# Attention in a hybrid decoder block: rounded values beside their remainder stationary, turned probabilities of two heads moving in two parts, sums turned back per four heads

## The chip, the cores and the metric

One Trainium2 chip, one core. The metric is device time in microseconds of one execution of the whole kernel, on the slowest (here the only) core. Three runs of the kernel before took 1873.67, 1875.36 and 1880.94 us; the median is 1875.36.

## What is computed

One decoder layer over a sequence of 1024 tokens and 1024 channels, in float32. Two token mixers run side by side: NSA (8 query heads, 2 key heads: a compressed branch, a branch over selected blocks, a sliding window of 512) and DSA (8 query heads, one key head, an indexer that keeps the top 256 keys). The change touches three of their products, probabilities times values, and how their result comes to the merge. The reference, cut to that:

```python
# NSA, per chunk of 64 queries; head dimension d = 64
p = masked_softmax(einsum('bqhgd,bqhkd->bqhgk', q_c, k_sel) * scale, sel_mask)      # "slc"
o_slc = einsum('bqhgk,bqhkd->bqhgd', p, v_sel)
p = masked_softmax(einsum('bqhgd,bkhd->bqhgk', q_c, kwin) * scale, win_mask)        # "win"
o_win = einsum('bqhgk,bkhd->bqhgd', p, vwin)
y_a = g0 * o_cmp + g1 * o_slc + g2 * o_win
# DSA                                                                             # "dsa"
y_b = einsum('bqhk,bqkd->bqhd', masked_softmax(einsum(q_c, k_sel) * scale, mask), v_sel)
merged = gate_a * (y_a @ w_branch_nsa) + gate_b * (y_b @ w_branch_dsa)
h = h + merged @ w_out
h = h + (silu(rmsnorm(h) @ w_gate) * (rmsnorm(h) @ w_up)) @ w_down
```

## The kernel before

The program is written per engine, with semaphores between them; nothing is planned by a tool, the order is that of the loops. It has these stages: normalise and project x (`z_step`, column groups idx, qb, cmp, win, qa, eight tiles of 128 tokens each), the indexer's scores and VectorE's bisection for the top keys, the merge gates' projection, the attention stage (about 495 to 946 us of the profiled span), the branch projections and merge (`m_step`, 16 steps of 24 products), the output projection, and the feed-forward part in two halves of the tokens.

**Number forms.** Wide products are made exact by splitting an operand: its rounding to the fast form F32R ("hi", always on ScalarE) and the remainder ("lo", on VectorE or GpSimd), each an operand of its own. `three` multiplies hi by hi, hi by lo and lo by hi. Where an operand is plain F32, one product is recorded as two passes.

**The attention stage** is one loop over steps u, run by each engine with its own part of each step. Its units are (branch, query tile i, head h), eight heads of a tile in a row: first all dsa tiles, then for each tile win and slc; 192 units. A unit works on n key blocks of 128: n = i + 1 for dsa and slc, at most 5 for win. In step u

- TensorE transposes the probabilities of unit u - 2 (`T_LAG`), 128 x 128 blocks, up to four into one of two PSUM banks (`group`, banks psT 0 and 1; line 1082 in `turn4`), makes the scores of unit u (lines 1141 and 1142, in psA), and multiplies the turned probabilities of unit u - 3 (`V_LAG`) by the values: probabilities stationary, 64 columns of values moving, plain F32 (line 1257), into an accumulator bank per tile (psT 2 and 3).
- ScalarE makes the exponential of unit u - 1 with its row sum (line 971) and copies the first turned bank out (`evac_p`, line 508); VectorE copies the second, if n > 4, and makes scores plus bias with the row minimum (line 1647, tile `s`).
- After the eighth head VectorE divides by the row sums (`scaled`, line 1675); for win and slc GpSimd adds that to the tile's y (line 798), which the compressed branch has begun (`cmp_out`, line 1682). At `Y_LAG` = 7 TensorE turns y, ScalarE rounds it (line 961), VectorE makes the remainder (line 1706): yTh and yTl, the operands of `m_step`.

`group` waits, before it writes a bank, until what was turned into it two groups ago has been taken out. The compressed branch (`cmp_tile`) runs along: its scores, softmax, output and the ranking of blocks (lines 1613 to 1630 on VectorE, the block bias on GpSimd) fall in fixed steps from slc of one tile to win of the next, and use the same two banks. In step 36 TensorE makes the compression products, 14.4 us in a row, in both kernels.

**Around it.** `z_evac` (ScalarE) takes each projection out of PSUM, `rope_cos` (GpSimd, line 705) multiplies by cosines, `rope` (VectorE, lines 1474 and 1479) by sines and adds. SyncE issues all loads in one order: queries two tiles ahead, the first weights of the merge (ring w2, two raw buffers, four split ones), then, after the last product and all banks taken, the gates, further weights and the gain. ScalarE splits two of these weights during the attention (`W2_AT`). `m_step(0)` runs near the end of the loop, the others after it; step m takes weight column block m // 2 and half m % 2 of the tokens.

## Time and profile before

| | us |
|---|---|
| median of three runs | 1875.36 |
| the runs | 1873.67 to 1880.94 |
| profiled execution: span from first to last instruction | 1870.0 |
| TensorE busy in the span | 1777.7 (95%) |
| VectorE | 837.2 (45%) |
| ScalarE | 672.4 (36%) |
| GpSimd | 584.2 (31%) |
| attention stage, first score to last value product | about 495 to 946 |

The profiled execution has no time of its own beside the runs; its span, 1870.0 us, is 5.4 under their median, and all rows below are read from it. How to read them: PE is TensorE's matmuls, PEld its weight loads, DVE is VectorE, ACT ScalarE, POOL GpSimd. A row of the timeline gives the start within the span, the duration, engine, line of the kernel, operation, output <- inputs, the form and how many such instructions are merged into the row; in brackets how long the engine had been idle and what released it. Matmuls are pipelined: a row's duration is longer than its distance to the next start, and the distance is what it costs. A window gives each engine's busy time in it and the granted TensorE clock as a share of 2.4 GHz (0.5 is the lower level, 1.2 GHz). The chain of waits is followed back from the last instruction, each step to what released it.

### The profile page before, as it was taken

The page shows a single profiled execution, that of the slowest core. Times are in us where ns is not written, and L with a number is a line of the kernel's source. Part 1 is how long each engine was busy: PE and PEld are TensorE (multiplying, and loading weights), DVE is VectorE, ACT ScalarE, POOL GpSimd, SP SyncE. Part 2 cuts the span into 40 slices and gives each one's busy share as a digit, 9 for nine tenths or more (in the row PEclk, how much of TensorE's full clock was granted, in tenths as well). Part 3 has the DMA queues.
Part 4 walks back from the last instruction along what each step waited for, and adds up shares of the span by engine and source line. Part 5 has one row for each costly group of instructions (what it writes and reads, how often), then busy time and mean ns, then how long its engine had stood idle before and what let it go on. Part 6 is the DMA issues. An engine that isn't in the chain of part 4 may idle for free.

```text
span 1870.0 us, 25106 instructions
## 1 busy us (share of the span) xinstructions
PE 1777.7 (95%) x9596; PEld 1526.2 (82%) x9596; DVE 837.2 (45%) x1796; ACT 672.4 (36%) x1310; POOL 584.2 (31%) x366
## 2 busy tenths in 40 slices
PE   6789979999999999999999989999999999999997
PEld 5667768888898999899988878888888888888886
DVE  6689788999135545566646322111131012311102
ACT  5543333221355467655522023322222223222222
POOL 3303233221220011321122024454454444544541
PEclk9899999999999989999999999999999999999999
DMA  5103232532422001001044223333333333433331
GB/s 175 45 12 103 80 96 86 174 90 74 113 64 113 24 29 30 12 17 31 1 130 141 80 85 96 91 100 103 90 102 102 101 90 90 140 105 93 101 102 68
DMA packets 179462, 158.01 MB, mean 84 GB/s; under 512 B 16912, under 2 KB 145936, under 8 KB 179088
## 3 DMA queue, kind: packets, MB, share of 16 engines
q1 hardware_dynamic: 179344, 156.41, 27.4%
q8 instruction: 77, 1.26, 0.3%
q14 instruction: 41, 0.34, 0.1%
HBM read 131.22 MB, written 25.17 MB: 84 GB/s over the span
## 4 chain that ended last, share of the span: by engine, by line
PE 84%; DVE 8%; ACT 3%; issue 2%; POOL 2%; DMA 1%; SPq 0%; DVEq 0%; ACTq 0%; POOLq 0%
PE psA L1075 18%; PE psA L1077 18%; PE psA L1076 18%; PE psT L1257 9%; PE psT L1082 7%; PE psA L1142 3%; PE psA L1141 3%; PE psT L1075 2%; PE psT L1077 2%; PE psT L1076 2%; POOL w_lo L319 1%; DVE rotated L1474 1%; DVE equal L1534 1%; DVE above L1534 1%; PE psT L1266 1%
## 5 line engine op out<-in xcount | busy, mean ns | idle before, releaser
L319 POOL TENSOR_TENSOR w_lo<-w_raw,w_hi 128x1024 fp32r<-128x1024 f32 (+2 forms) x184 | 453.6, 2479 | 657.4 <-ACT w_hi L314 657.4
L314 ACT CAST w_hi<-w_raw 128x1024 fp32r<-128x1024 f32 (+2 forms) x184 | 186.6, 1038 | 660.4 <-PE psA L1077 525.9
L1075 PE MATMUL psA<-hTh,w_hi 128*128 128x512 f32 x704 | 273.9, 389 | 0.2 <-POOL w_lo L319 0.2
L1076 PE MATMUL psA<-hTl,w_hi 128*128 128x512 f32 x704 | 273.9, 389 | 0.0
L1077 PE MATMUL psA<-hTh,w_lo 128*128 128x512 f32 x704 | 273.9, 389 | 0.0
L1820 DVE TENSOR_TENSOR act<-silu,psA 128x512 f32<-128x512 f32 x44 | 30.2, 687 | 393.5 <-ACT silu L1046 393.5
L971 ACT ACTIVATE p<-s,nmax 128x640 f32<-128x640 f32 (+7 forms) x192 | 144.0, 750 | 120.3 <-DVE nmax L1647 119.1
L1075 PEld LDWEIGHTS psA<-hTh,w_hi 128*128 128x128 f32 x704 | 132.1, 188 | 28.2 <-issue 0.6
L1076 PEld LDWEIGHTS psA<-hTl,w_hi 128*128 128x128 f32 x704 | 132.1, 188 | 27.4
L1077 PEld LDWEIGHTS psA<-hTh,w_lo 128*128 128x128 f32 x704 | 132.1, 188 | 27.2
L1082 PE MATMUL psT<-ident,p 128*128 128x128 f32 x816 | 131.0, 281 | 18.8 <-DVE yTl_dsa L1706 4.7
L1075 PE MATMUL psA<-w_hi,xTh 128*128 128x512 f32 (+2 forms) x320 | 123.5, 386 | 14.2 <-POOL w_lo L319 10.0
L1082 PEld LDWEIGHTS psT<-ident,p 128*128 128x128 f32 x816 | 98.4, 153 | 25.9 <-ACT p L971 6.4
L1077 PE MATMUL psA<-w_hi,xTl 128*128 128x512 f32 (+2 forms) x320 | 119.2, 372 | 0.0
L1076 PE MATMUL psA<-w_lo,xTh 128*128 128x512 f32 (+2 forms) x320 | 119.0, 372 | 0.0
L508 ACT COPY pT<-psT 128x512 f32<-128x512 f32 (+3 forms) x192 | 93.8, 488 | 20.6 <-PE psT L1082 20.1
L1075 PE MATMUL psA<-xTh,w_hi 128*128 128x512 f32 x256 | 100.0, 391 | 0.0
L1077 PE MATMUL psA<-xTh,w_lo 128*128 128x512 f32 x256 | 99.6, 389 | 0.0
L1076 PE MATMUL psA<-xTl,w_hi 128*128 128x512 f32 x256 | 99.6, 389 | 0.0
L1534 DVE TENSOR_SCALAR_CACHE_REDUCE equal<-score,bit_try 128x512 f32<-128x512 f32 (+2 forms) x93 | 93.8, 1008 | 0.0
L705 POOL TENSOR_TENSOR roped<-z,cosT 128x512 f32<-128x512 f32 (+3 forms) x48 | 40.7, 854 | 161.8 <-ACT z L846 96.1
L1075 PEld LDWEIGHTS psA<-w_hi,xTh 128*128 128x128 f32 x320 | 61.5, 192 | 26.1 <-POOL w_lo L319 12.6
(259 smaller groups left out, 3544.4 us busy)
## 6 DMA issues: line engine op xcount, KB each, us to landing
w_raw<-in_w_gate_dram SPq DMA_DIRECT2D x44, 512.0 KB, 3.8
w_raw<-in_w_up_dram SPq DMA_DIRECT2D x44, 512.0 KB, 3.9
w_raw<-in_w_down_dram SPq DMA_DIRECT2D x44, 512.0 KB, 3.8
w_raw<-in_w_in_dram SPq DMA_DIRECT2D x28, 512.0 KB, 3.9
scratch_gates<-gate_out SPq DMA_DIRECT2D x32, 256.0 KB, 2.9
gates<-scratch_gates SPq DMA_DIRECT2D x32, 256.0 KB, 4.1
xr<-in_x_dram SPq DMA_DIRECT2D x8, 512.0 KB, 4.9
scratch_q_dsa<-turned SPq DMA_DIRECT2D x8, 512.0 KB, 2.6
```

Of the source, the lines that this page charges most:

```text
L314: nc.scalar.copy(self.hi[n % RING][:, 0:u], self.raw[n % RAW][:, 0:u]).then_inc(self.hi_done, 1)
L319: nc.gpsimd.tensor_tensor(self.lo[n % RING][:, 0:u], self.raw[n % RAW][:, 0:u], self.hi[n % RING][:, 0:u].bitcast(F32), ALU.subtract).then ...
L508: copy(pT[v % 2][:, c0 // P:c1 // P, :].rearrange("p k t -> p (k t)"), psT[:, g6[key] % 2, 0:c1 - c0])\
L971: a_.activation(p_sb[v % PR][:, 0:n], s_sb[v % 2][:, 0:n], ACT.Exp, scale=-1.0, bias=nmax[:, BR[a], i, h:h + 1], accum_out=psum_p[:, BR[a] ...
L1075: pe.matmul(ps, ah, bh, start=first, stop=False)
L1076: pe.matmul(ps, ah, bl, start=False, stop=False)
L1077: mm = pe.matmul(ps, al, bh, start=False, stop=last)
L1082: mm = pe.transpose(bank[:, P * n:P * (n + 1)], src, ident[:])
L1141: pe.matmul(ps[:, c0:c1], q_, k_hi[:, c0:c1], start=True, stop=False)
L1142: mm = pe.matmul(ps[:, c0:c1], q_, k_lo[:, c0:c1], start=False, stop=True)
L1257: mm = pe.matmul(bank[:, HD * h:HD * (h + 1)], pT[v % 2][:, k, :], val, start=(k == 0), stop=(k == n - 1))
L1534: done.append(signal(v_.tensor_scalar((tk_gt, tk_eq)[n % 2][:, 0:P * (i + 1)], score_of(i), threshold(n), None, ALU.is_ge, ALU.add, accum_ ...
```

## The change

- **Values.** v_b, v_slc and v_win hold, beside each other, 64 columns of the rounded value and 64 of its remainder, in F32R. ScalarE writes the rounded part as it takes the projection out (and copies 128 columns more into z in the cmp and win groups); GpSimd subtracts, ahead of its cosine product.
- **Probabilities.** The exponential is written over the scores; there are six such buffers instead of two and three. Two heads (a pair) are turned together: a job is up to two key blocks of both, four transposes. ScalarE writes the rounded copy (512 columns in F32R), VectorE the remainder from the same bank, after it. Jobs of a pair fall on steps u + 3 and u + 4 of its second head, the first half of them (rounded up) on the first.
- **Product.** One step after its job: for each key block the values are stationary (128 columns, both parts), the pair's 256 columns of rounded, then of remainder probabilities move. The accumulator, a bank for four heads (a group), holds 64 rows of each part by 4 x 128 queries.
- **Turning back.** Six steps after a group's last head ScalarE copies the accumulator to SBUF, TensorE turns it in four transposes into bank 0 or 1, VectorE scales it in the next step, ahead of that step's jobs, and GpSimd adds the two parts (and adds that to y for win and slc). y is turned at lag 8.
- **y of tiles 4 to 7** is only copied (y_raw, ScalarE); rounded and remainder parts are made at the end, in four pieces for each mixer. `m_step` takes the first half of the tokens for three column blocks first (`MSEQ`); steps 0 and 1 stand in the loop; a third weight is split early.
- Buffers are laid out anew; SyncE loads the gates once the last compressed output has been taken and the last block scores are made.

The diff, cut to its core:

```diff
-    E_LAG, T_LAG, V_LAG, F_LAG, Y_LAG = 1, 2, 3, 4, 7
+    E_LAG, T_LAG, V_LAG = 1, 3, 1
+    O_LAG, F_LAG, Y_LAG = T_LAG + 1 + V_LAG + 1, T_LAG + 1 + V_LAG + 2, 8
+    M_AT = [len(units) + T_LAG, len(units) + O_LAG, len(units) + Y_LAG + 1]
+    MSEQ = [(j, 0) for j in range(3)] + [(j, 1) for j in range(3)]
+    MSEQ += [(j, half) for j in range(3, KT) for half in range(2)]
+    for u in range(1, len(units), 2):
+        a, i, h = units[u]
+        n = keys_of(a, i)[1]
+        mine = [(u, k, min(2, n - k)) for k in range(0, n, 2)]
+        first = (len(mine) + 1) // 2
+        for m, job in enumerate(mine):
+            jobs_at[u + T_LAG + (m >= first)].append(len(jobs))
+            jobs.append(job)
...
@@ GpSimd, rope_cos @@
+            for v, col, n in VALUES.get(c, []):
+                nc.gpsimd.tensor_tensor(value[:, :, HD:2 * HD], heads(zs[q % 2][:, col:col + n * HD], n),
+                                        value[:, :, 0:HD].bitcast(F32), ALU.subtract)
...
@@ GpSimd, attention @@
+            if group_of(u, F_LAG):
+                pool.wait_ge(t_dve, dve_took["o", a, i, g])
+                if a == "dsa":
+                    nc.gpsimd.tensor_tensor(y, part[0], part[1], ALU.add).then_inc(y_done, 1)
+                else:
+                    then(nc.gpsimd.tensor_tensor(part[0], part[0], part[1], ALU.add))
+                    nc.gpsimd.tensor_tensor(y, y, part[0], ALU.add).then_inc(y_done, 1)
...
@@ ScalarE, attention, in this order within a step @@
+            if group_of(u, O_LAG):
+                act.wait_ge(pj_done, last_job[key] + 1)
+                a_.copy(acc[o % 2][:], psT[:, 2 + o % 2, :]).then_inc(acc_out, 1)
             if y_of(u - 1):
+                if i < HT:
+                    a_.copy(yTh[set_, 0][:, :, tok(i)], ps).then_inc(yh_done, 1)
+                else:
+                    a_.copy(y_raw[set_][:, :, tok(i - HT)], ps).then_inc(t_act, 1)
+            for j in jobs_at[u]:
+                act.wait_ge(t_ps, g6["p", j, 0] + 1)
+                a_.copy(pT[j % PT][0][:, 0:w], psT[:, g6["p", j, 0] % 2, 0:w]).then_inc(ph_done, 1)
-                a_.activation(p_sb[v % PR][:, 0:n], s_sb[v % 2][:, 0:n], ACT.Exp, scale=-1.0,
+                a_.activation(s_sb[v % SR][:, 0:n], s_sb[v % SR][:, 0:n], ACT.Exp, scale=-1.0,
...
@@ TensorE, attention @@
+            for j in jobs_at[u]:
+                pe.wait_ge(p_done, uq + 1)
+                turn4(group(("p", j, 0)), [s_sb[v % SR][:, P * c:P * (c + 1)] for c in range(k, k + nk) for v in (uq - 1, uq)])\
+                    .then_inc(t_ps, 1)
+            for j in jobs_at[u - V_LAG]:
+                pe.wait_ge(t_dve, dve_took["p", j, 0])
+                for c in range(k, k + nk):
+                    pe.matmul(bank, val, pT[j % PT][0][:, cols], start=(c == 0), stop=False)
+                    mm = pe.matmul(bank, val, pT[j % PT][1][:, cols], start=False, stop=(c == n - 1))
-                    mm = pe.matmul(bank[:, HD * h:HD * (h + 1)], pT[v % 2][:, k, :], val, start=(k == 0), stop=(k == n - 1))
+            if group_of(u, O_LAG):
+                pe.wait_ge(acc_out, o + 1)
+                turn4(group(("o", *opened[o])), [acc[o % 2][:, P * k:P * (k + 1)] for k in range(G)]).then_inc(t_ps, 1)
+            if u == M_AT[1]:
+                m_step(1)
...
@@ VectorE, attention, ahead of unit_scores(u) @@
+            if group_of(u, F_LAG):
+                scaled(*group_of(u, F_LAG))
+            for j in jobs_at[u]:
+                dve.wait_ge(ph_done, j + 1)
+                v_.tensor_tensor(pT[j % PT][1][:, 0:w], psT[:, g6["p", j, 0] % 2, 0:w], pT[j % PT][0][:, 0:w].bitcast(F32),
+                                 ALU.subtract).then_inc(t_dve, 1)
...
@@ SyncE @@
-        sp.wait_ge(pv_ps, len(units))
-        sp.wait_ge(t_dve, len(dve_took))
+        sp.wait_ge(t_dve, dve_took["co", NT - 1, 0])
+        sp.wait_ge(bs_done, NT - TOPN // 2)
```

## Rows read from the trace of the kernel before

**Rows 1.** Of the page: busy time, share of the span and instructions of each engine.
```profile
PE 1777.7 (95%) x9596; PEld 1526.2 (82%) x9596; DVE 837.2 (45%) x1796; ACT 672.4 (36%) x1310; POOL 584.2 (31%) x366
```

**Rows 2.** Windows: PE, PEld, DVE, ACT, POOL busy us, granted clock, DMA share, GB/s.
```profile
495.00:504.00 9.00, 7.72 (x40) 7.46 (x41) 2.73 (x18) 6.53 (x26) 0.62 (x2) 0.62 0.69 46
504.00:512.00 8.00, 7.17 (x61) 6.68 (x59) 4.34 (x18) 6.78 (x25) 7.77 (x7) 1.00 1.09 344
667.00:677.00 10.00, 10.00 (x56) 9.96 (x56) 5.23 (x23) 5.45 (x25) 3.32 (x3) 0.53 0.09 22
800.00:950.00 150.00, 144.85 (x1162) 137.26 (x1162) 88.60 (x200) 75.90 (x150) 26.73 (x41) 1.00 0.04 12
```

**Rows 3.** Chain of waits, stretches of the attention: start us, us, what.
```profile
506.01 0.39 PE psT L1257 x4
...
507.90 0.39 PE psT L1257 x4
...
530.77 0.84 PE psT L1257 x8
...
532.52 0.84 PE psT L1257 x8
...
785.42 1.11 PE psT L1257 x10
787.73 1.11 PE psT L1257 x10
...
927.17 1.73 PE psT L1257 x16
930.71 1.73 PE psT L1257 x16
```

**Rows 4.** Timeline, a dsa unit of eight key blocks: start us, us, engine, line.
```profile
639.09 1.04 PE L1082 MATMUL psT<-ident,p 128*128 128x128 f32 x8
...
639.89 0.48 PE L1141 MATMUL psA<-kbT,q 128*128 128x512 f32 x1
...
640.90 1.89 PE L1257 MATMUL psT<-v_b,pT 128*128 128x64 f32 x16
```

**Rows 5.** Timeline, TensorE: score products of 256 columns, and 280 columns in the projection.
```profile
505.73 0.28 PE L1142 MATMUL psA<-kbT,q 128*128 128x256 f32 x1
...
505.85 0.33 PE L1257 MATMUL psT<-v_b,pT 128*128 128x64 f32 x2
...
238.26 0.29 PE L1076 MATMUL psA<-w_lo,xTh 128*128 128x280 f32 x1
238.39 0.29 PE L1077 MATMUL psA<-w_hi,xTl 128*128 128x280 f32 x1
```

**Rows 6.** Timeline, the last turn of y, until the product that waits for it.
```profile
951.94 0.60 PE L1082 MATMUL psT<-ident,ya 128*128 128x128 f32 x4
952.58 0.58 ACT L961 CAST yTh_nsa<-psT 128x512 fp32r<-128x512 f32 x1 [9.37 <-PE psT L1082]
...
953.19 0.69 DVE L1706 TENSOR_TENSOR yTl_nsa<-psT,yTh_nsa 128x512 fp32r<-128x512 f32 x1 [5.87 <-ACT yTh_nsa L961]
...
953.94 0.50 PE L1075 MATMUL psA<-yTh_nsa,w_hi 128*128 128x512 f32 x1 [1.40 <-DVE yTl_nsa L1706]
```

**Rows 7.** Timeline, VectorE: a subtraction and what follows it.
```profile
520.97 0.69 DVE L1706 TENSOR_TENSOR yTl_dsa<-psT,yTh_dsa 128x512 fp32r<-128x512 f32 x1 [1.11 <-ACT yTh_dsa L961]
521.58 0.55 DVE L1647 CUSTOM_DVE_ANT_0 s<-psA,score 128x384 f32<-128x384 f32 x1
```

**Rows 8.** Instructions of lines 1647 and 971: ns min/median/max, first and last start.
```profile
L1647 DVE CUSTOM_DVE_ANT_0 s<-psA,slc_bias x32: 823/1024/1225, 776.3 to 937.9; 128x640 f32<-128x640 f32 x8, 128x768 f32<-128x768 f32 x8, 128x896 f32<-128x896 f32 x8, 128x1024 f32<-128x1024 f32 x8
...
L971 ACT ACTIVATE p<-s,nmax x192: 385/779/1154, 496.4 to 939.2; 128x640 f32<-128x640 f32 x48, 128x128 f32<-128x128 f32 x24, 128x256 f32<-128x256 f32 x24, 128x384 f32<-128x384 f32 x24
```

**Rows 9.** Timeline, VectorE at the start of a win tile.
```profile
755.73 0.42 DVE L1613 TENSOR_TENSOR cmp_above<-blk_score 128x256 f32<-128x256 f32 x1 [1.11 <-POOL blk_score L758]
```

**Rows 10.** Timeline, GpSimd in the window projection.
```profile
237.72 0.53 POOL L705 TENSOR_TENSOR roped<-z,cosT 128x128 f32<-128x128 f32 x1 [2.89 <-DVE blocks L1491]
```

More of the change, by code:

```diff
@@ L275, in hybrid_block @@
     M_STEPS, O_STEPS, F_STEPS = 2 * KT, 2 * NT, FT
[L276 removed]
+    free2 = m_last + [M_STEPS + 8 * (n // 4) + 7 for n in range(8)]
     for t in range(2):
@@ L462, in hybrid_block @@
             w1.gone.append((g_ps, 2 * (n - NCH) + 2))
-    w2.gone = [(m_ps, 2 * j + 2) for j in range(KT)]
+    w2.gone = [(m_ps, m + 1) for m in m_last]
     frees = 0
@@ L935, in _, with chunks_hi @@
             a_.activation(gst[g % 2][:], psA[:, g % 4, :], ACT.Sigmoid).then_inc(g_out, 1)
+        def chunks_hi(set_):
+            act.wait_ge(pj_done, len(jobs))
+            act.wait_ge(t_act, act_took["y", "dsa" if set_ == "dsa" else "slc", NT - 1])
+            for k in range(KT // 2):
+                a_.copy(yTh[set_, 1][:, k, :], y_raw[set_][:, k, :]).then_inc(yc_hi, 1)
         for u in range(STEPS6):
```

299 lines of the change are left out of this document (158 added, 141 removed).

## The prediction

> **What bounds the kernel now.** TensorE is the busy engine [rows 1]. I read the windows by stage first: the attention stage, about 495 to 946 us, is the only one that the change touches much, and in its long tiles TensorE is busy 145 of 150 us at the full clock, VectorE 89, ScalarE 76 [rows 2]. Short tiles differ: in 495 to 504 and 667 to 677 us the granted clock is 0.62 and 0.53, near its lower level. The chain of waits then gives the time of one unit (a head of a query tile with n key blocks) as the distance between two groups of value products: 3.54 us for n = 8, 2.31 for 5, 1.75 for 4, 0.95 for 2 (two units, 506.01 to 507.90) [rows 3]. By the timeline the unit of n = 8 is 0.80 us of transposes, 1.01 of scores and 1.73 of value products, one behind the other [rows 4]: nothing but TensorE's own work, so what leaves TensorE is gained, as long as the others keep up.
>
> **Value products, the gain.** One product costs 1.73/8 = 0.216 us; there are 816 (36 blocks x 8 heads in dsa and in slc, 30 x 8 in win): 176 us. After, a block of two heads takes two products of 256 columns, again 816. No row has this product with values stationary. The nearest is the score product of 256 columns, next start 0.12 us on; the bounds are 0.108 (a product of today is recorded as two passes, 16 in 1.73 us: a weight load and 64 columns each) and 0.13 (280 columns) [rows 4, 5]. I take 0.12, so 98 us, -78 (-88 to -70). The page "TensorE: Matmul & The Clock Gate" of the Trainium skill, section "Back-to-back issue gap", gives N/2.4 + 2.5 ns, 109 ns for 256 columns; by it the sum would be 9 us lower, but the rows lie above its rule.
>
> **Turning back, a cost.** 48 groups x 4 transposes, 0.40 to 0.44 us a group as the turn of y takes: +21 us. Work alone says -57 us. The rest of the working is what stands against it.
>
> **A new round trip.** Each job (up to 4 transposes) is now rounded by ScalarE and then subtracted by VectorE before its bank is free and its product may start. The turn of y at the end of the stage is just this trip: transposes at 951.94, rounding 952.58, subtraction 953.19, next product 953.94, 2.0 us in all [rows 6]. Before, products ran one step behind their transposes, with one copy between. Now:
> n = 2: one job per pair; between its transposes and its product TensorE has only two scores (0.5 us) and waits. A pair takes 2.0 + 4 x 0.12 = 2.48, 1.24 us a unit against 0.95.
> n = 1: a job half as wide, 1.35 + 0.24 = 1.6 a pair, 0.80 a unit, against 0.96 at the low clock now.
> n = 3: again 2.0 + 0.48, 1.25 a unit against 1.3.
> n = 4: one job a step; transposes, scores, products 0.44 + 0.46 + 0.48 = 1.38 against 1.75; the trip of 2.0 ends before the next step's product, at 2.28, is due.
> n = 5: jobs of 4, 4 and 2 transposes, two in the even step, one in the odd. Work 1.80 + 1.86 a pair, and the third job waits 0.29 for the first one's bank (free at 0.65 + 0.59 + 0.69 and a start, 2.09; wanted at 1.80): 3.95, 1.98 a unit against 2.31. n = 6, 7, 8: 2.10, 2.42 and 0.80 + 1.01 + 0.96 = 2.77, against 2.7, 3.1, 3.54 (the first two between the rows of 5 and 8).
> VectorE carries it: at n = 8 two subtractions and a score pass. A subtraction lasts 0.69, but the next operation begins 0.61 later [rows 7]; the score pass holds 1.15 of its 1.22 (0.82 at n = 5) [rows 8]. That is 2.37 of 2.77 us. ScalarE has two roundings of 0.59 and an exponential of 1.15 [rows 6, 8]: 2.33. Neither binds in the mean, and both have little left. (In all, ScalarE's 192 copies become 232 roundings and 48 accumulator copies; VectorE's 96 copies become 232 subtractions, and its scalings go from 24 to 48. The walks hold them.)
>
> **The queue in front of the turn back.** The turned group holds one of two banks until VectorE's scaling, which stands behind the score pass of the step before. Walk of a step with n = 8, from its first transpose: accumulator copied by ScalarE from 0.3, first rounding 0.8 to 1.4, subtractions from 1.4 and 2.0, score pass 2.6 to 3.8, scaling to 4.5. TensorE ends its products at 2.77 and the turn at 3.21, does the next job by 3.65, and the job after waits for the bank until 4.6. A group costs 0.44 + 0.95 = 1.39. The same walk gives 1.27 for n = 7 and 1.32 for 6 (scaling 5.14 to 5.83, wait until 5.95 instead of 5.07). For 5 the job waits from 4.83 to 5.21, and the third job of the next pair no longer waits its 0.29: 0.53. For 4 the step after the turn needs the bank of the last job, held up by the accumulator copy (free 2.38, wanted 1.82), and the scaling then delays the one after: 1.0. For 3 it is 0.66, for 2 and 1 the turn alone, 0.44, since TensorE waits there anyhow. The waits alone, two groups a tile over the 24 tiles, come to 20 us. The page "Vector Engine: DVE Perf Modes" of the Trainium skill, section "The DRAIN you can't avoid", says that the next operation starts only when the pipe is empty; with 0.69 for each subtraction instead of 0.61 a group would wait some 0.2 to 0.3 longer, 8 to 12 us in all; the row speaks against it.
>
> **Sum of a tile** (8 units, 2 groups), after less before: n = 1 +1.5 (taken at the mixed clock that it has now), 2 +3.2, 3 +0.9, 4 -1.0, 5 -1.5, 6 -1.8, 7 -2.9, 8 -3.3. The y of tiles 4 to 7 is only copied by ScalarE, no subtraction before its bank is free: -0.7 in each of four dsa and four slc tiles. dsa: -4.9 - 2.8 = -7.7; slc the same; win (1 to 4, then four times 5): -1.4. Together -17.
>
> **The compressed branch.** Its PE work is unchanged, but its ranking puts some 4 us on VectorE within three steps of each win tile from 4 on (compares of 0.42 in a row, and a 1.1 us wait for GpSimd ahead of them) [rows 9]. Now VectorE has over a microsecond a step to spare, then 0.4 to 0.5: about 2.5 us of backlog x 4 tiles reaches TensorE, and some 0.5 in the rest: +11 (3 to 20).
>
> **Front and end.** GpSimd makes the values' remainder ahead of the cosine product. In the window projection the chain goes through it every second step (product 237.72, 0.53 long [rows 10], sum and blocks behind it): 0.4 x 4; beside it 0.4 for the rest: +2 (0 to 5). In the index projection VectorE's sine products run longer than GpSimd, no cost. After the attention the merge begins with the first half of the tokens, and the wait of 1.40 us behind the last y [rows 6] can go; but TensorE waits newly for the last accumulator copy (0.21 + 0.59 + 0.1 = 0.9), and merge step 3 waits for the second half: last turn of y, copy 0.8, four roundings and remainders, 4.0 us, then the merge of step 1, three operations of 0.61, 5.9 us in all against 5.5 of products of step 2. With the turn that makes +0.5 (-2 to +3). SyncE now loads the gates once the last compressed output is taken, not after the whole attention; behind them stand w_branch loads, then the gain, which waits for the last turn, then the next gates, which wait for a merge step anyway. Earlier gates free VectorE, which TensorE isn't waiting for. The third early split of a weight (ScalarE and GpSimd at two steps past the last unit) has both engines to itself. The new order of the buffers and the smaller scratch for descriptors: none.
>
> Sum: -17 + 11 + 2 + 0.5 = -3.5 us, against the profiled span of 1870.0: 1866.5. The median of three runs, 1875.36, lies 5.4 over that span, and I take that distance as kept: 1871.9.
>
> **Rivals.** (1) The banks don't hold TensorE: VectorE sees the turned group early, since the score pass is over when it comes, and the ranking is absorbed. For it: VectorE has 2.37 of 2.77 us, and before it shows long idle. Against it: program order puts scaling behind the score pass. Then the 20 us of waits go, and some of the 11: 1871.9 - 20 - 5 = 1847.
> (2) Slower: in short tiles the clock stays at its lower level. Now it does so in n = 1 and n = 2 tiles [rows 2], with TensorE issuing without a gap; after, it issues there just over half of the time. At half speed a pair of n = 2 or 3 takes 3.4 us instead of 2.5: 48 units x 0.46 = +22, 1894. It decides if the granted clock of the tiles n = 2 and 3 is under 0.75. Against it: 504 to 512 us ran at 1.00.
> (3) VectorE binds in the nsa tiles: the backlog is twice what I took, +13: 1885.
> (4) The product does not get cheaper: at 0.16 instead of 0.12, as when a weight load of values isn't hidden, +33: 1905. Nothing in the rows speaks for it.
>
> **How the numbers follow.** My forecast 1871.9 has 0.38, with a range of its own of 1862 to 1882 (walks good to 0.05 us a unit, 10 us); rival 1 0.33; rival 2 0.15; rival 3 0.12; rival 4 0.02. The 8 in 10 reach from 1842 to 1898: below lies a quarter of rival 1, above two fifths of rival 2 and rival 4. Faster by over 0.5% (9 us, about what a measurement of this kernel tells from no change) is rival 1 and a tenth of the forecast, 0.37; slower are rivals 2 to 4 and a bit, 0.30; within 0.5%, 0.33.
>
> **What would show it.** Right: the new products start 0.12 us apart; units of n = 8 come every 2.8 us but one in four 1.4 later, with TensorE waiting for the scaling; n = 2 tiles last 10 to 11 us against 7.6, TensorE waiting for VectorE's subtraction; the attention stage ends within 10 us of now; VectorE is busy some 85% of the n = 8 windows. Wrong: no wait on the scaling (rival 1), a clock under 0.75 for 40 us or more (rival 2), VectorE without idle at the win tiles (rival 3). It fails most easily in the sum of small terms of both signs: 0.1 us a unit is 19 us.

## The result

| | before | changed |
|---|---|---|
| median of four runs | 1876.94 us | 1912.72 us (1910.19 to 1914.78) |
| ratio, with its 95% interval | 1 | 1.0188 (1.0173 to 1.0204) |
| profiled span | 1870.0 us | 1911.2 us |
| forecast | | 1871.9 us (1842 to 1898) |

The change makes the kernel 1.9% slower. The forecast said no measurable change, and the time lies above its range. The four runs of the kernel before are the three that the forecast started from and one more. The span grows by 41.2 us and the median by 35.8: the traced execution of the kernel before was a quick one. In every run for which both are known the time is 1.7 to 2.1 us over the span, so that execution took some 1871.9 us, 5 under the median of its kernel. Comparisons of the two traces below therefore show up to some 5 us too much in sum.

The busy line of the page, changed kernel (answers [rows 1]):
```profile
PE 1753.2 (92%) x8972; PEld 1475.7 (77%) x8972; DVE 948.8 (50%) x1956; ACT 727.8 (38%) x1406; POOL 632.3 (33%) x454
```
TensorE is busy 24.5 us less and the span is 41.2 us longer: some 66 us of idle time are new. The windows show where (columns as in [rows 2]): first a stretch early in the indexed tiles, then the indexed tile of eight key blocks, then the tiles slc0 (one block) and slc1 (two).
```profile
507.20:537.70 30.50, 10.85 (x55) 9.34 (x54) 7.49 (x26) 8.27 (x25) 24.72 (x31) 0.61 0.58 181
...
638.80:666.90 28.10, 25.07 (x185) 22.62 (x184) 22.74 (x42) 19.58 (x37) 3.48 (x4) 1.00 0.06 20
682.50:693.90 11.40, 9.32 (x57) 8.31 (x57) 7.13 (x30) 6.46 (x24) 4.15 (x5) 0.77 0.11 36
707.10:721.10 14.00, 11.64 (x77) 10.15 (x76) 9.14 (x30) 8.05 (x24) 4.38 (x6) 0.88 0.16 50
```
In the first stretch TensorE works 10.85 of 30.5 us while GpSimd (fifth busy figure) works 24.72. In the kernel before, TensorE works 24.92 of the 26 us from 504 to 530.

The waits of TensorE between 500 and 975 us, changed kernel, name what each waits for: total, times, longest.
```profile
PE psT L1147 <- POOL ya L835: 17.6, 1, 17.6
PE psT L1147 <- DVE ytmp L1739: 17.2, 23, 1.7
PE psT L1321 <- DVE pT_lo L1805: 11.6, 20, 0.9
PE psT L1147 <- DVE ya L1747: 11.0, 8, 2.4
PE psT L1147 <- DVE pT_lo L1805: 9.4, 11, 2.3
```
Line 1147 is the turning (probabilities, sums, y), 1321 the first of the two products; `ya L835` is GpSimd's adding of the two parts of the sums, `ytmp L1739` VectorE's scaling, `pT_lo L1805` VectorE's subtraction, and `ya L1747` VectorE's taking the output of the compressed branch out of its bank.

To place the loss I compare the start of VectorE's first score pass of each tile in the two kernels (a tile named dsa4 is the indexed branch, query tile 4, of five key blocks). "Lag" is changed less before.

| from | before | changed | lag |
|---|---|---|---|
| dsa0 | 495.7 | 500.6 | +4.9 |
| dsa2 | 512.0 | 537.7 | +25.7 |
| win0 (end of indexed) | 653.0 | 666.9 | +13.9 |
| win4 | 753.8 | 780.9 | +27.1 |
| slc7 | 915.5 | 947.8 | +32.3 |
| first product of the feed-forward part | 1135.9 | 1177.1 | +41.2 |

Four places: the front (+4.9), one stall in dsa1 (its length 8.6 us before, 30.4 now), the nsa tiles (+18.4 from win0 to slc7), and the end (+8.8). The indexed tiles without the stall give back 9. The stall is counted as 18.1 us: dsa1 takes 30.4, and 12.3 in the first run below, which removes it.

### The profile page after: what moved, and what is told of

Read it like the earlier page. It is cut to its first block, busy times and chain, and to the rows that moved or that the text cites. A ratio compares the mean times of both kernels' runs of the same rounds, so it can differ in the third digit from the quotient of the medians.

```text
span 1911.2 us, 24079 instructions
## 1 busy us (share of the span) xinstructions
PE 1753.2 (92%) x8972; PEld 1475.7 (77%) x8972; DVE 948.8 (50%) x1956; ACT 727.8 (38%) x1406; POOL 632.3 (33%) x454
## 4 chain that ended last, share of the span: by engine, by line
PE 74%; DVE 10%; issue 6%; POOL 4%; ACT 4%; DMA 1%; SPq 0%; DVEq 0%; POOLq 0%; ACTq 0%
PE psA L1140 18%; PE psA L1142 18%; PE psA L1141 18%; PE psT L1147 6%; PE psT L1140 2%; PE psT L1142 2%; PE psT L1141 2%; PE psT L1321 2%; PE psA L1207 2%; PE psA L1206 2%; PE psT L1322 1%; POOL w_lo L334 1%; DVE s L1717 1%; DVE equal L1604 1%; ACT pT_hi L1030 1%
## 5 line engine op out<-in xcount | busy, mean ns | idle before, releaser
L1805 DVE TENSOR_TENSOR pT_lo<-psT,pT_hi 128x512 fp32r<-128x512 f32 (+1 forms) x232 | 141.9, 624 | 87.5 <-ACT pT_hi L1030 85.9
L1147 PE MATMUL psT<-ident,s 128*128 128x128 f32 x816 | 130.5, 283 | 39.3 <-DVE ytmp L1739 17.2
L1030 ACT CAST pT_hi<-psT 128x512 fp32r<-128x512 f32 (+1 forms) x232 | 121.9, 538 | 113.8 <-PE psT L1147 112.0
L1036 ACT ACTIVATE s<-s,nmax 128x640 f32<-128x640 f32 (+7 forms) x192 | 145.2, 756 | 14.2 <-DVE nmax L1717 13.3
L1140 PE MATMUL psA<-w_hi,xTh 128*128 128x512 f32 (+2 forms) x320 | 124.8, 390 | 14.1 <-POOL w_lo L334 10.0
L1147 PEld LDWEIGHTS psT<-ident,s 128*128 128x128 f32 x816 | 93.7, 144 | 56.2 <-issue 48.5
L1140 PEld LDWEIGHTS psA<-w_hi,xTh 128*128 128x128 f32 x320 | 62.8, 196 | 25.6 <-POOL w_lo L334 11.9
## 6 DMA issues: line engine op xcount, KB each, us to landing
w_raw<-in_w_gate_dram SPq DMA_DIRECT2D x44, 512.0 KB, 3.8
w_raw<-in_w_up_dram SPq DMA_DIRECT2D x44, 512.0 KB, 3.8
w_raw<-in_w_down_dram SPq DMA_DIRECT2D x44, 512.0 KB, 3.8
w_raw<-in_w_in_dram SPq DMA_DIRECT2D x28, 512.0 KB, 3.9
xr<-in_x_dram SPq DMA_DIRECT2D x8, 512.0 KB, 4.7
scratch_q_dsa<-turned SPq DMA_DIRECT2D x8, 512.0 KB, 2.6
```

What stands on the lines that cost most here:

```text
L1030: a_.copy(pT[j % PT][0][:, 0:w], psT[:, g6["p", j, 0] % 2, 0:w]).then_inc(ph_done, 1)
L1036: a_.activation(s_sb[v % SR][:, 0:n], s_sb[v % SR][:, 0:n], ACT.Exp, scale=-1.0, bias=nmax[:, BR[a], i, h:h + 1], accum_out=psum_p[:, BR[a ...
L1140: pe.matmul(ps, ah, bh, start=first, stop=False)
L1147: mm = pe.transpose(bank[:, P * n:P * (n + 1)], src, ident[:])
L1805: v_.tensor_tensor(pT[j % PT][1][:, 0:w], psT[:, g6["p", j, 0] % 2, 0:w], pT[j % PT][0][:, 0:w].bitcast(F32), ALU.subtract).then_inc(t_dve, 1)
```

## Experiments

Every kernel below is an edit of the changed kernel, timed beside the kernel before; ratios are to that kernel, so the changed kernel's 1.0188 is what each is to be held against.

**GpSimd's queue.** GpSimd works in program order. In the kernel before VectorE wrote the sums of the indexed tiles itself, and GpSimd came to its attention loop whenever it liked. In the changed kernel it adds the two parts of these sums, and its loop stands behind the compressed branch's window additions and constants. From the changed kernel's timeline (the additions of the windows, the last of the constants, the first sums, and the turning that waits for them):
```profile
508.38 10.38 POOL L528 TENSOR_TENSOR cmp_x_k<-kcvcT,cmp_pos_k 64x504 f32<-64x504 f32 x8
...
519.04 10.18 POOL L528 TENSOR_TENSOR cmp_x_v<-kcvcT,cmp_pos_v 64x504 f32<-64x504 f32 x8
...
532.72 0.19 POOL L708 TENSOR_SCALAR_AFFINE_SELECT row_sees_window<-row_sees_window 128x1 f32<-128x1 f32 x1
532.99 1.40 POOL L835 TENSOR_TENSOR ya<-ytmp 128x256 f32<-128x256 f32 x2
534.44 1.11 PE L1147 MATMUL psT<-ident,ya 128*128 128x128 f32 x4 [17.64 <-POOL ya L835]
```
The edit gives the windows out one by one, with the constants after them:
```diff
-        for n, done in ((0, cx_k), (1, cx_v)):
-            made(pool.memset(xc[n][:, :, :, NW:64], 0.0))
-            windows(nc.gpsimd, n, done)
...
         for u in range(STEPS6):
...
+            if 9 <= u <= 25:
+                if u >= 10:
+                    pool.wait_ge(y_done, sum(bool(group_of(w, F_LAG)) for w in range(u + 1)))
+                next(window_list, None)
+            if u == 26:
+                setup()
```


> The changed kernel with GpSimd's 16 window additions for the compressed branch (21 us in one piece at 508 to 529) given out one per unit of the indexed branch, from its tenth unit on, and its constants (3.7 us) after them, so that the additions of the sums of a query tile no longer stand behind them. Theory A (GpSimd's queue holds the first turned sum, and TensorE with it, 17.6 us): the wait of 17.6 us ahead of TensorE's first turning of a finished tile goes, the second indexed tile takes 11 to 13 us and not 30.4, and the time is 1893 to 1897 us. Rival (the stall only holds work that is short of something else behind it, the loaded queries or the lower clock of the short tiles, and shows up there again): the tiles of two and three blocks grow by what the stall loses and the time stays over 1905 us.

Measured: 1895.56 us, ratio 1.0093 (1.0076 to 1.0110), 17.2 us less. dsa1 takes 12.3 us and not 30.4, and every later tile keeps its length within about 2 us. Its timeline shows the sums of a tile between window additions, with no long wait:
```profile
506.84 0.73 POOL L846 TENSOR_TENSOR ya<-ytmp 128x256 f32<-128x256 f32 x1 [0.24 <-DVE ytmp L1757]
507.65 5.39 POOL L533 TENSOR_TENSOR cmp_x_k<-kcvcT,cmp_pos_k 64x504 f32<-64x504 f32 x4
513.12 0.74 POOL L846 TENSOR_TENSOR ya<-ytmp 128x256 f32<-128x256 f32 x1
```
The stall is GpSimd's queue. The rival, that something behind it was late anyway, falls.

**SyncE's queue at the end.** In the changed kernel VectorE waits 7.5 us for the gates of the third merge step, and TensorE behind it 4.4 us:
```profile
997.53 0.37 SPq L322 DMA_DIRECT2D w_raw<-in_w_branch_nsa_dram  x1
...
998.49 0.50 SPq L655 DMA_DIRECT2D gain<-in_norm_ffn_dram  x1
...
999.04 9.99 SPq L647 DMA_DIRECT2D gates<-scratch_gates  x6
...
1006.19 0.69 DVE L1769 TENSOR_TENSOR ma<-psA,gates 128x512 f32<-128x512 f32 x1 [7.54 <-DMA gates<-scratch_gates]
...
1008.35 0.76 PE L1140 MATMUL psA<-yTh_nsa,w_hi 128*128 128x512 f32 x1 [4.41 <-DVE merged L1774]
```
The buffer of those gates is free once the first merge step is out, at 984.1. The load is issued at 999.04, because SyncE has a weight load in front of it, and this waits for GpSimd's split of the chunk before (995.11 to 997.50), which waits for ScalarE's rounding at 993.99, which stands behind the last y.
```diff
-        for n in range(2 * RAW, RAW + RING):
+        w2.load(sp, 2 * RAW)
+        sp.wait_ge(m_done, 1)
+        load_gates(2)
+        for n in range(2 * RAW + 1, RAW + RING):
             w2.load(sp, n)
```


> The changed kernel with the third load of gates put ahead of the weight load that waits for GpSimd's splitting, and ahead of the gain. Theory D (SyncE's queue has this load behind a weight load that waits for a split, and it lands at 1006 where its products are ready at 998): VectorE's wait of 7.5 us for gates goes and the time falls by 6 to 8 us, to 1905 to 1907 us. Rival (the split of the weights behind the last product is what the merging step waits for, with or without its gates): less than 2 us are won, the time is over 1910.5 us and the wait stands against the weights.

Measured: 1905.33 us, ratio 1.0149 (1.0134 to 1.0164), 7.4 us less, although TensorE's own wait was 4.4 us. The gates are now issued at 985.37, and the same merge step starts at 999.77:
```profile
985.37 0.81 SPq L647 DMA_DIRECT2D gates<-scratch_gates  x2
...
999.77 0.68 DVE L1772 TENSOR_TENSOR ma<-psA,gates 128x512 f32<-128x512 f32 x1
```
The granted clock seems to be the rest. Windows of the same 20 us, the changed kernel and this one:
```profile
1000.00:1020.00 20.00, 15.59 (x60) 12.33 (x59) 10.88 (x11) 3.25 (x4) 4.78 (x2) 0.83 0.51 168
...
1000.00:1020.00 20.00, 20.00 (x89) 16.42 (x88) 13.78 (x15) 5.02 (x6) 7.22 (x3) 1.00 0.67 210
```
A share of 0.17 over 20 us is 3.4 us, and 4.4 and 3.4 are close to the 7.4 won.

**The bank of the turned sums.** The turned sums take one of the two banks that the turned probabilities use in turn, and hold it until VectorE has scaled them. But the accumulator bank that they were copied from lies empty. The edit turns them back into that one:
```diff
-            groups6.append(("o", *opened[-1]))
...
             if first and o >= 2:
-                pe.wait_ge(acc_out, o - 1)
+                pe.wait_ge(o_scaled, o - 1)
...
-                turn4(group(("o", *opened[o])), [acc[o % 2][:, P * k:P * (k + 1)] for k in range(G)]).then_inc(t_ps, 1)
+                turn4(psT[:, 2 + o % 2, :], [acc[o % 2][:, P * k:P * (k + 1)] for k in range(G)]).then_inc(o_back, 1)
```


> The changed kernel with the sums of four heads turned back into the PSUM bank from which they were copied, and no longer into one of the two banks that the turned probabilities take in turn. Theory B (the two banks are short: TensorE's waits for the scaling, 17.2 us in 23 places, are waits for a bank): the waits for the scaling go, the nsa tiles lose 8 to 17 us in sum and the time is 1896 to 1905 us. Rival (TensorE would next wait for the same VectorE, whose score pass and subtraction are late by as much): the waits move to the subtraction of the turned probabilities or to the score pass, and the time is over 1909 us.

Measured: 1890.18 us, ratio 1.0069 (1.0054 to 1.0084), 22.5 us less, more than either theory gave. No wait of TensorE for the scaling is left between 500 and 975 us. What is left of the same view:
```profile
PE psT L1147 <- POOL ya L835: 18.3, 2, 17.5
PE psT L1321 <- DVE pT_lo L1804: 13.2, 24, 0.9
PE psT L1147 <- DVE pT_lo L1804: 8.0, 9, 1.9
```
dsa6 goes from 22.1 to 20.1 us, win4 from 27.2 to 23.9, slc7 (to its last score pass) from 19.4 to 17.3; the nsa tiles up to slc7 take 269.9 us in sum instead of 280.9. In win4 the granted clock changes too. Its window in the changed kernel and in this one:
```profile
780.90:808.10 27.20, 20.04 (x133) 18.31 (x134) 20.06 (x43) 15.00 (x32) 12.83 (x18) 0.87 0.00 1
...
771.20:795.20 24.00, 17.85 (x134) 16.25 (x135) 19.86 (x44) 15.10 (x33) 12.89 (x18) 1.00 0.00 1
```
So some of what this edit wins beyond the waits may be clock. The page "Perfetto Trace Analysis" of the Trainium skill, section "Matmuls", asks that groups of products rotate through different banks, so that one is emptied under the next. The run agrees: with the turned sums out of the rotation, the 17.2 us of waits for the scaling are gone. In this kernel a group that is emptied late (behind a score pass) is best kept out of a rotation of two.

**One unit more of lag.** If the trip over ScalarE and VectorE holds the products, they should come a step later.
```diff
-    E_LAG, T_LAG, V_LAG = 1, 3, 1
-    O_LAG, F_LAG, Y_LAG = T_LAG + 1 + V_LAG + 1, T_LAG + 1 + V_LAG + 2, 8
+    E_LAG, T_LAG, V_LAG = 1, 3, 2
+    O_LAG, F_LAG, Y_LAG = T_LAG + 1 + V_LAG + 1, T_LAG + 1 + V_LAG + 2, 9
```


> The changed kernel with the value products one unit later behind the turning of their probabilities, so that rounding and subtraction have a unit's time more. Theory F (the round trip over ScalarE and VectorE holds the products: TensorE waits 29.3 us for the subtraction in 39 places between 500 and 975): these waits shrink to under 10 us, most of it in the tiles of one to three blocks, and the time falls by 8 to 20 us, to 1893 to 1905 us. Rival (VectorE or the bank is late by as much anyway): the waits stand at the turnings instead, and the time is 1909 to 1916 us.

Measured: 1952.7 us, ratio 1.0406 (1.0385 to 1.0426): 40 us slower, outside both expectations. By tile it is two results. The tiles of one and two blocks got shorter (win1 13.2 to 11.0, slc1 14.0 to 11.7), but for win0 behind the long dsa7 (15.6 to 19.3); the long ones got much longer (dsa7 28.1 to 41.6, win7 24.7 to 35.2). A wait shows why, ScalarE's before its rounding, between 500 and 975 us:
```profile
ACT pT_hi L1030 <- PE psT L1322: 95.9, 53, 5.1
```
In the changed kernel no such wait for line 1322 is listed. The ring of turned, rounded jobs has four places (`PT`). With two jobs a step and a lag of two, all four are waiting for products, and the next rounding waits for a place, under program order on three engines. This reads as the trip costing the short tiles, and the ring limiting the cure.

**Remainders behind the cosine.** For the front I moved GpSimd's remainders of the values behind its cosine products.
```diff
-            for v, col, n in VALUES.get(c, []):
...
             last.then_inc(cos_done, 1)
+            for v, col, n in VALUES.get(c, []):
...
+                last.then_inc(vlo_done, 1)
```


> The changed kernel with GpSimd's remainders of the values put behind its cosine products of the same projection step, and no longer ahead of them. Theory E (the remainders delay the rotation of queries and keys, 24 steps, and with it the projections: the gate stage starts 4.9 us later than in the kernel before): the gate stage starts 3 to 5 us earlier than in the changed kernel and the time falls by 3 to 5 us, to 1908 to 1910 us. Rival (the copies on ScalarE and the length of GpSimd's work at each step are what is late, whatever their order): less than 1.5 us are won, over 1911 us.

Measured: 1908.84 us, ratio 1.0175 (1.0155 to 1.0196), whose interval holds the changed kernel's ratio. So both were run again side by side.

> The changed kernel itself, beside the one with the remainders behind the cosine, on one chip and in the same rounds, because the start of the first indexed tile lay between 497.5 and 501.5 us in five profiled kernels with the same front, which is as much as theory E is to explain. 1909 to 1916 us; the first score pass of the first indexed tile again between 497 and 502 us.

> The remainders of the values behind the cosine, as before, in five rounds beside the changed kernel. Theory E: 3 to 5 us under the changed kernel of this same call. Rival (the front's start moves by such amounts from execution to execution, whatever the order): within 1.5 us of it.

Measured: the changed kernel 1912.34 us, the edited one 1913.32 us, ratios 1.0185 (1.0165 to 1.0205) and 1.0184 (1.0163 to 1.0205). The edit moves the time by less than these runs tell, and the expectation that it wins 3 to 5 us falls. The first score pass of dsa0 lay at 500.6, 497.5, 501.5, 498.0, 499.6, 497.9, 498.1 and 498.9 us in the eight profiled kernels without this edit (mean 499.0), and at 495.9, 499.0, 496.8, 498.9 and 498.6 in the five with it (mean 497.8). One value, 495.7, stands for the kernel before. Much of this scatter goes with the granted clock in the front. Per 100 us up to 300 it is 0.93, 0.97 and 0.98 in the kernel before (495.7), in two of the kernels without the edit (498.1 and 498.0) and in two with it (495.9 and 496.8); the three latest starts (499.6, 500.6 and 501.5) are those with 0.93 from 200 to 300 us. So at the same clock the changed front is some 2.3 us longer, and the edit may give 1 to 2 us of it back, which is less than the medians can tell. The rest of the +4.9 is the clock of the execution that was traced.

**Four edits together.** Windows, gates, bank and remainders in one kernel, with no other change.

> Four edits together on the changed kernel: the windows given out, the gates loaded ahead, the sums turned back into their own bank, and the remainders behind the cosine. If each acts on a place of its own (17 + 7.4 + 22.5 us measured one by one, and 3 to 5 for the last if theory E holds), the time is 1861 to 1866 us, under the kernel before. Rival (two of them free the same stretch: the freed bank lets TensorE run on to a wait that another edit left): the gains add to under 42 us and the time is over 1871 us.

Measured: 1866.77 us, ratio 0.9941 (0.9920 to 0.9962). The three edits that act gave 17.2 + 7.4 + 22.5 = 47.1 us singly and 46.0 together: three separate places, and the remainders none. That the time lies just above the stated 1861 to 1866 is the 3 to 5 us that the remainders did not bring. This kernel is 0.6% faster than the kernel before.

**The longer lag for short tiles only.**
```diff
-    E_LAG, T_LAG, V_LAG = 1, 3, 1
-    O_LAG, F_LAG, Y_LAG = T_LAG + 1 + V_LAG + 1, T_LAG + 1 + V_LAG + 2, 8
+    E_LAG, T_LAG, V_LAG = 1, 3, 2
+    O_LAG, F_LAG, Y_LAG = T_LAG + 1 + V_LAG + 1, T_LAG + 1 + V_LAG + 2, 9
...
+            values_at[step + (V_LAG if n <= 4 else 1)].append(len(jobs))
...
-            for j in jobs_at[u - V_LAG]:
+            for j in values_at[u]:
```


> The four edits together, and the value products a unit later, but only in tiles of one to four key blocks (where the lag of two made the tiles of one and two blocks shorter by 0.8 to 2.3 us each), with the lag of one in the longer tiles (where the lag of two let the ring of four turned pairs run full and cost up to 13.5 us a tile). Theory F (the round trip is what makes the short tiles longer than before): they lose 10 to 18 us in sum and the time is 1845 to 1858 us. Rival (what they lose at the products they wait at the bank or for the score pass): within 4 us of the kernel with the four edits.

Measured: 1848.83 us, ratio 0.9853 (0.9836 to 0.9870), 17.9 us under the kernel of the four edits and 27.5 under the kernel before. The nsa tiles of one to four blocks give 11.4 of it (slc0 12.2 to 9.6 us, win1 13.3 to 10.6, win3 14.4 to 12.8). The edit does a second thing: through `O_LAG`, `F_LAG` and `Y_LAG` the turning back of the sums and of y comes one step later in every tile, the long ones too. dsa7 goes from 26.5 to 24.8 us and win4 from 24.0 to 22.5, whose products kept the lag of one. No run separates the two. Windows of this kernel, dsa7, slc0 and slc1:
```profile
611.90:636.70 24.80, 24.42 (x184) 22.66 (x182) 22.02 (x41) 19.07 (x37) 3.49 (x4) 1.00 0.07 22
650.60:660.30 9.70, 7.55 (x57) 6.34 (x56) 6.94 (x30) 6.65 (x25) 3.74 (x5) 1.00 0.02 5
670.90:682.50 11.60, 10.30 (x74) 8.47 (x74) 9.56 (x31) 8.30 (x24) 4.54 (x6) 1.00 0.12 28
```
The long tile is filled with TensorE's work, 24.42 of 24.80 us.

> The kernel of the mixed lags with the longer lag taken back from the indexed tiles of three and four blocks, which were 1.2 and 2.7 us longer with it than in the kernel of the four edits. If the lag is the reason, 3 to 4 us are won, 1844 to 1847 us; if it was where their score passes fell against the windows that GpSimd and VectorE work on, there is no difference (within 1.5 us of 1848.8 us).

The edit is `V_LAG if n <= (2 if a == "dsa" else 4) else 1`. Measured: 1848.67 us, 0.9855 (0.9838 to 0.9871): no difference. dsa3 is shorter (15.3 to 13.0 us) and dsa2 longer (14.1 to 15.3): the two together 28.3 instead of 29.4, so the lag accounts for 1 us there at most, and not for the 3.9 by which I had them.

**What is TensorE's own time worth?** The prediction took its gain from cheaper products. Two kernels leave work out to price it.
```diff
-                    pe.matmul(bank, val, pT[j % PT][0][:, cols], start=(c == 0), stop=False)
-                    mm = pe.matmul(bank, val, pT[j % PT][1][:, cols], start=False, stop=(c == n - 1))
+                    mm = pe.matmul(bank, val, pT[j % PT][0][:, cols], start=(c == 0), stop=(c == n - 1))
```


> The changed kernel without the 408 products of the values with the remainders of the probabilities (the subtraction on VectorE stays and is still waited for; the sums lack what these products give). It asks what TensorE's own time is worth in the attention. If TensorE sets the length of the tiles of four and more blocks (336 of these products, 0.12 us each) as the prediction had it, the time falls by 336 x 0.12 = 40 us at most, by 30 to 40 us likely, to 1873 to 1883 us. Rival (VectorE's slots or the two banks set it): under 15 us are won, over 1898 us, and VectorE's spacing of the score passes stays.

Measured: 1905.53 us, ratio 1.0159 (1.0144 to 1.0174): 7.2 us (5.4 by the ratios) from 408 products that lasted 49. dsa7, from which 32 x 0.12 = 3.8 us of TensorE's work went, is 0.6 us shorter. Its window:
```profile
633.00:660.50 27.50, 22.14 (x153) 18.88 (x151) 22.49 (x41) 19.44 (x37) 3.45 (x4) 1.00 0.07 21
```
TensorE has 2.9 us less busy time than in the changed kernel (its matmul records overlap, so the difference of busy times is less than the work taken out), VectorE is as before with 22.49, and the tile is nearly as long. The clock hides part of the gain elsewhere: in this execution slc4 ran at 0.84 instead of 1.00 and took 21.8 us instead of 20.0. So I also take the six tiles that ran at 1.00 in both kernels (dsa3 to dsa7 and slc6): 148 products, 17.8 us, went from them, and they are 3.6 us shorter in sum (140.0 to 136.5).
```diff
             for j in jobs_at[u]:
-                dve.wait_ge(ph_done, j + 1)
-                v_.tensor_tensor(pT[j % PT][1][:, 0:w], psT[...], pT[j % PT][0][...], ALU.subtract).then_inc(t_dve, 1)
...
-                pe.wait_ge(t_dve, dve_took["p", j, 0])
+                pe.wait_ge(t_act, act_took["p", j, 0])
```


> The changed kernel without the products with the remainders of the probabilities, and also without VectorE's subtractions that make them (216 of 512 or 256 columns, up to 0.69 us each), so that a product waits for ScalarE's rounding alone and a bank is free after it; the sums lack what the remainders give. Leaving out the products alone won 7 us. If VectorE's turn (its slots, the bank that it holds, the second half of the round trip) is what sets the attention where the prediction had TensorE, the time falls by 35 us and more, to under 1878 us, and the long tiles get shorter by 2 to 5 us each. Rival (ScalarE or TensorE's sequencer is the next limit right behind): under 15 us below the kernel without the products, over 1890 us.

Measured: 1860.67 us, ratio 0.9911 (0.9891 to 0.9932), 44.9 us below the kernel without the products. dsa7 is 24.5 us, slc5 17.8 instead of 22.1, and the six tiles at the full clock 122.6 instead of 136.5:
```profile
624.40:648.90 24.50, 20.94 (x150) 18.53 (x149) 13.50 (x24) 18.57 (x36) 3.47 (x4) 1.00 0.06 22
```
So in the changed kernel it is VectorE's part that sets the attention: its slots, the banks it holds, and the second half of the trip, which this kernel takes away together (GpSimd's stall and the late gates are still in its time). The two edits of order share it out in part, 22.5 us for the bank of the sums and 17.9 for the longer lags. With both, and with every subtraction and product in place, dsa7 takes 24.8 us, nearly what it takes here; slc5 takes 21.7 (20.2 in the run after it) and not 17.8. What divides that rest between VectorE's slots and the trip was not tried.

## Why the prediction was wrong, step by step

The forecast for the profiled span was 1866.5 us; the span is 1911.2. Of the 44.7 us between them the tiles' starts place 44.4 (lags are rounded):

| step | forecast | traces | missed by | test |
|---|---|---|---|---|
| dsa tiles | -7.7 | -9.1 | -1.4 | |
| stall in dsa1 | none | +18.1 | +18.1 | -17.2 when the windows are given out |
| nsa tiles up to slc7, with the compressed branch | +5.9 | +18.4 | +12.5 | -11.0 with the bank edit, -12.4 more with the lags |
| slc7 and the end | -3.5 | +8.8 | +12.3 | -7.4 for the gates |
| front | +2 | +4.9 | +2.9 | +2.3 at the same clock; no effect of the order on the time |

The distance from span to median came out at 1.5 instead of 5.4 us, which takes 3.9 off: 40.8. That 5.4 was to be kept was wrong: it belonged to one quick execution and not to the kernel. The error made the miss smaller, by luck.

**The failed step: a queue that was not walked.** The prediction costs GpSimd's remainders in the front and its third split at the end, and says nothing of the adding that moved to it. The row was there: in 504 to 512 us of the kernel before GpSimd is busy 7.77 of 8.00 us with seven instructions [rows 2], and the row was read for TensorE's clock only. A moved operation enters a queue in program order, and what stood ahead of it was 21 us of windows and 3.7 of constants, while the first sums were scaled by VectorE at 509.14. The term was put at nothing without a reason. This is the largest single part of the miss, and it was measured at 17.2 us; with it gone the time, 1895.56 us, would lie within the range that was given, still 24 us over the forecast.

**Products (right).** They start 0.12 us apart in the changed kernel; the timeline of TensorE in slc1 (answers [rows 5]):
```profile
713.01 0.28 PE L1322 MATMUL psT<-pT_lo,v_win 128*128 128x256 f32 x1
713.13 0.28 PE L1321 MATMUL psT<-pT_hi,v_win 128*128 128x256 f32 x1
713.25 0.28 PE L1322 MATMUL psT<-pT_lo,v_win 128*128 128x256 f32 x1
```
Rival 4 falls. The 109 ns that the page "TensorE: Matmul & The Clock Gate" of the Trainium skill, section "Back-to-back issue gap", gives for a single product are not reached here, where starts are 120 ns apart; the trace decides.

**"Neither binds in the mean" (wrong, the second failed step).** The length of n = 8 was right: dsa7 takes 28.1 us against a forecast of 31.2 - 3.3 = 27.9. The reason was not. The timeline of VectorE in a step of dsa7 in the changed kernel (answers [rows 4]):
```profile
660.09 1.22 DVE L1717 CUSTOM_DVE_ANT_0 s<-psA,score 128x1024 f32<-128x1024 f32 x1
661.23 0.08 DVE L1717 DVE_READ_ACCUMULATOR2_ANT nmax<- 128x1 f32 x1
661.23 0.20 DVE L1671 RECIPROCAL c_st<-c_st 128x8 f32<-128x8 f32 x1
661.46 0.23 DVE L1672 TENSOR_SCALAR c_st<-c_st,row_sees_window 128x8 f32<-128x8 f32 x1
661.80 1.29 DVE L1805 TENSOR_TENSOR pT_lo<-psT,pT_hi 128x512 fp32r<-128x512 f32 x2
...
663.00 1.22 DVE L1717 CUSTOM_DVE_ANT_0 s<-psA,score 128x1024 f32<-128x1024 f32 x1
```
and of the same step without the remainder products:
```profile
653.77 1.22 DVE L1716 CUSTOM_DVE_ANT_0 s<-psA,score 128x1024 f32<-128x1024 f32 x1
...
655.29 1.28 DVE L1804 TENSOR_TENSOR pT_lo<-psT,pT_hi 128x512 fp32r<-128x512 f32 x2
...
656.48 1.22 DVE L1716 CUSTOM_DVE_ANT_0 s<-psA,score 128x1024 f32<-128x1024 f32 x1
```
VectorE works through this step with hardly a gap, 2.91 us with all products and 2.71 without half of them, where TensorE's work is 0.80 + 1.01 + 0.96 = 2.77 and 0.48 less. The small operations of the compressed branch, which the walk of a unit left out, fill what I had called spare. One step is not the tile, though: over all of dsa7 VectorE is busy 22.74 of 28.10 us (81%, the forecast said some 85%), and in eight places, 4.2 us in sum, it waits for ScalarE's rounding. The longest step, between the score passes at 655.63 and 660.09 (rows below), takes 4.46 us, and 4.45 without the remainder products. There one thing stands behind another: VectorE's scaling, TensorE's turning into the bank that it frees, ScalarE's rounding, VectorE's subtraction, the score pass. None of these is a product with the values. The walk had VectorE busy for 2.37 of 2.77 us a unit; measured it is 2.84 of 3.51, small operations and scalings included. So the length comes from VectorE's share together with the trip, and time taken off TensorE's products is worth little: 0.6 of 3.8 us, as measured. The sum counted all of it and laid single waits on top. Rival 3, that VectorE binds, held in part in the long tiles too, where the text had it only for the ranking.

**Waits for the scaling (right, and worth more).** 20 us were walked, 17.2 in 23 places measured, with the score pass ahead of it as told, and here a reduction of the compressed branch besides. The longest, in dsa7 of the changed kernel:
```profile
655.63 1.22 DVE L1717 CUSTOM_DVE_ANT_0 s<-psA,score 128x1024 f32<-128x1024 f32 x1
...
656.77 0.68 DVE L1666 TENSOR_REDUCE c_st<-c_p 128x8 f32<-128x512 f32 x1
657.36 0.68 DVE L1739 TENSOR_TENSOR ytmp<-psT,psum_r 128x512 f32<-128x512 f32 x1
...
658.19 0.63 PE L1147 MATMUL psT<-ident,s 128*128 128x128 f32 x4 [1.71 <-DVE ytmp L1739]
...
658.86 0.59 ACT L1030 CAST pT_hi<-psT 128x512 fp32r<-128x512 f32 x1 [1.75 <-PE psT L1147]
...
659.48 0.69 DVE L1805 TENSOR_TENSOR pT_lo<-psT,pT_hi 128x512 fp32r<-128x512 f32 x1 [0.83 <-ACT pT_hi L1030]
```
So rival 1 (1847) does not hold. Its price of 25 us is close to the 22.5 that the bank edit wins; why that is more than the waits' own 17.2 was not taken apart; the clock in win4, shown with that run, is one part that the traces show.

**Short tiles (right).** The sum has n = 6 at -1.8, where its own figures (2.10, 2.7 and twice 1.32) give -2.2; that changes little. A pair of n = 2 was walked at 2.48 us. In the changed kernel, slc1, VectorE's subtraction comes 0.73 us after VectorE is free, and TensorE waits 0.55 us for it:
```profile
711.82 0.41 PE L1207 MATMUL psA<-kT_slc,q 128*128 128x256 f32 x1
712.79 0.39 PE L1321 MATMUL psT<-pT_hi,v_win 128*128 128x256 f32 x1 [0.55 <-DVE pT_lo L1805]
...
712.04 0.69 DVE L1805 TENSOR_TENSOR pT_lo<-psT,pT_hi 128x512 fp32r<-128x512 f32 x1 [0.73 <-ACT pT_hi L1030]
```
The nsa tiles of one to three blocks are 11.9 us longer in sum, where the forecast had 11.2 and 1.0 for the compressed branch (the 11 less four times 2.5). The miss lies in the longer ones: win3 to win7 were to win 7 us and lose 10 to the ranking, 3 in all, and lost 9.6; slc3 to slc6 were to win 9.3 and won 3.0. One wait there was in no walk: TensorE stands for VectorE's taking the compressed branch's output out of its bank, 3.0 us in five places before and 11.0 in eight now (`ya L1747`); 7.1 are left with the mixed lags.

**The clock (rival 2, not as told, but not nothing).** It was to be decided by the tiles of two and three blocks. But for dsa1 with the stall, their granted clock in the changed kernel's trace is 0.94 in win1, 0.88 in slc1 and 0.97 to 1.00 in the three tiles of three blocks, all over 0.75. In the trace of its second run slc1 is at 0.67 and takes 15.7 us instead of 14.0, so a single tile can fall either way. In the first trace the clock also falls where TensorE has new waits: 0.61 in dsa1, where it stands still (0.84 with the windows given out, counted in the 17.2 us), 0.83 from 1000 to 1020 us behind the gates, and 0.87, 0.93 and 0.93 in win4, win5 and win6, which ran at 1.00 in the kernel before. No term of the sum had this.

**The end (wrong in one link).** "The next gates, which wait for a merge step anyway" is true of their buffer and not of the queue: the weight load ahead of them waited for a split behind the last y, over 13 us after the gates could have gone. That link alone was 7.4 us, with the clock behind it. The further 5 us lie in how the tiles are measured, I think: slc7 is 3.0 us shorter to its last score pass (22.4 to 19.4), and from there to the first product of the feed-forward part it is 198.0 us before and 203.0 with the gates ahead. The reason I give for it is not shown by a run: the probabilities of a pair are turned at three to four steps after its scores and not at two, so more products are left after slc7's last score pass, and what the tile seems to win is spent there.

## What to carry to other kernels

When an operation moves to another engine, list that engine's queue at the step where its first result is wanted, up to the setup work that nobody waited for until now; do the same for each load that stands behind a wait on SyncE. Before counting work taken off the busiest engine as won, see whether another engine's turn, with everything that stands in its queue and the trip between the two, is as long (here a step of 2.91 and one of 4.46 us beside 2.77 of TensorE's work): a kernel that leaves the work out prices this in one run. Keep a group that is emptied late out of a rotation of two banks, and choose the lag between a step and its use by tile length, within the places of the ring between them.

## What the runs showed of the hardware

In slc0, a tile of one block, the granted clock was 0.57 in the kernel before (10.00 us, TensorE busy throughout) and 0.77 in the changed kernel (11.40 us, busy 9.32). Two edited kernels that make the same products in it differ most: with the four edits 0.56 in 12.20 us, TensorE busy 11.55; with the mixed lags 1.00 in 9.70 us, busy 7.55. The busier TensorE was the slower one: at the lower level, 1.2 GHz, the same work counts as longer busy time (the 77 instructions of slc1 11.64 us at 0.88, 14.01 at 0.67 in the changed kernel's second run). So a high busy share was no sign of a high clock. What decides the level in this tile no run shows. I had expected more gaps to cost clock, if anything; behind the stall of 17.6 us and behind the late gates they did (0.61 and 0.83).

The place where the attention begins moved by up to 4 us between profiled kernels with the same front (497.5 to 501.5 us), and a good part of that went with the granted clock, while the medians of the changed kernel, from two sets of four runs, agreed within 0.4 us (1912.72 and 1912.34). Two single traces are no measure of a stage for 3 us.
